# First rows normed beside the modulation, GpSimd's pieces of the attention reordered, and the last norm scaled through a diagonal on TensorE

## What is computed

```python
m_lat = silu(c) @ w_mod + b_mod            # six vectors: sh1 sc1 g1 sh2 sc2 g2; m_ctx from c_ctx likewise
h = modulate(x, sh1, sc1)                  # (x - mean) / std * (1 + sc1) + sh1, context rows with their own
u, gate, q, k, v = split(h @ w_in)         # 512, 512, 512, 128, 128
r = rglru(conv(u));  a = window_attention(rope(q), rope(k), v, context keys, sink)
y = concat(rms_norm(r * gelu(gate)), rms_norm(a)) @ w_out
x1 = layer_norm(ALPHA * x + g1 * y, ln1);  h2 = modulate(x1, sh2, sc2)
out = layer_norm(ALPHA * x1 + g2 * moe(h2), ln2)   # 32 experts, top 1 group, top 2 experts
```

## Time and profile before

| what | value |
|---|---|
| median of 3 runs | 2081.2 us (2080.24 to 2082.03) |
| the profiled execution's own time | 2081.28 us |
| its span | 2079.5 us |
| TensorE matmuls / VectorE / ScalarE / GpSimd busy | 82% / 70% / 51% / 25% of the span |
| mean granted TensorE clock | 0.923 of full |
| projection, attention, output, route blocks start near | 68.9, 578.4, 829.4, 1082.9 us |
| combine block starts near | 2014.7 us |

### The profile page before, as it was taken

The page is one execution under the profiler, slowest core; times in us unless marked ns, Lnnn a source line. Parts: engine busy times, 40 slices in busy tenths (PEclk is TensorE's granted clock), DMA queues, the critical chain, the costliest instruction groups (busy, mean ns, idle before and its releaser), DMA issues. The chain is left out here.

```text
span 2079.5 us, 76106 instructions
## 1 busy us (share of the span) xinstructions
PE 1713.2 (82%) x31174; PEld 1373.2 (66%) x31176; DVE 1464.5 (70%) x1828; ACT 1066.5 (51%) x1378; POOL 526.5 (25%) x413
## 2 busy tenths in 40 slices
PE   3488888888669997899961689986899799999947
PEld 0266666434257776455541689986899799999932
DVE  2466766388869997788878747777888636578727
ACT  2234343577558886433311535566676435456626
POOL 0000000000047777333322113231323121233213
PEclk7599999999889999899975899998999899999979
DMA  9321211367363331344326576898999748879837
GB/s 375 104 92 56 96 60 52 129 229 259 122 251 124 115 121 40 125 153 159 136 91 223 196 242 206 266 361 316 352 373 342 263 137 280 270 228 368 272 77 278
DMA packets 167293, 412.59 MB, mean 198 GB/s; under 512 B 15977, under 2 KB 24625, under 8 KB 165553
## 3 DMA queue, kind: packets, MB, share of 16 engines
q1 hardware_dynamic: 155554, 369.14, 49.4%
q0 software_dynamic: 11664, 42.47, 8.3%
HBM read 343.38 MB, written 68.19 MB: 198 GB/s over the span
## 5 line engine op out<-in xcount | busy, mean ns | idle before, releaser
L2200 PE MATMUL ps<-arena 128*128 128x64 f16 x7680 | 708.5, 195 | 53.9 <-DVE arena L2121 25.7
L2200 PEld LDWEIGHTS ps<-arena 128*128 128x128 f16 x7680 | 686.5, 99 | 62.5 <-issue 50.4
L2201 PE MATMUL ps<-arena 128*128 128x64 f16 x7680 | 708.3, 195 | 4.7 <-issue 3.9
L2202 PE MATMUL ps<-arena 128*128 128x64 f16 x7680 | 708.2, 195 | 3.9 <-issue 3.0
L2201 PEld LDWEIGHTS ps<-arena 128*128 128x128 f16 x7680 | 686.2, 99 | 6.0 <-issue 5.0
L2202 PEld LDWEIGHTS ps<-arena 128*128 128x128 f16 x7680 | 686.3, 99 | 2.8 <-issue 2.7
L2121 DVE SCALAR_TENSOR_TENSOR arena<-arena 128x2048 f16<-128x2048 f32 (+1 forms) x232 | 457.6, 2012 | 162.9 <-ACT arena L2048 95.5
L2048 ACT ACTIVATE arena<-arena 128x2048 f16<-128x2048 f32 x192 | 359.0, 1904 | 126.3 <-DMA arena<-w 80.0
L644 PE MATMUL ps<-arena 128*128 128x256 f16 (+1 forms) x1680 | 237.7, 303 | 21.1 <-DVE arena L529 21.1
L644 PEld LDWEIGHTS ps<-arena 128*128 128x128 f16 x1680 | 165.8, 100 | 87.3 <-DVE arena L529 15.2
L2015 POOL COPY ix<-gidx 128x1 int32 (+1 forms) x40 | 47.0, 1176 | 531.3 <-DVE arena L2154 531.3
(11 more groups left out here) (308 smaller groups left out, 3107.6 us busy)
## 6 DMA issues: line engine op xcount, KB each, us to landing
arena<-w SPq DMA_DIRECT2D x192, 1024.0 KB, 12.0
arena<-hT_d SPq DMA_DIRECT2D x64, 512.0 KB, 6.2
arena<-w_mod SPq DMA_DIRECT2D x16, 1536.0 KB, 8.3
h_d<-arena SPq DMA_DIRECT2D x17, 512.0 KB, 3.0
x_d<-arena SPq DMA_DIRECT2D x17, 512.0 KB, 2.6
arena<-x SPq DMA_DIRECT2D x8, 1024.0 KB, 6.2
...
```

The costliest lines, as they stand in the source:

```text
L2200: pe.matmul(out, whi[lane][:, at:at + P], high, start=first, stop=False)
L2201: pe.matmul(out, whi[lane][:, at:at + P], low, start=False, stop=False)
L2202: return pe.matmul(out, wlo[lane][:, at:at + P], high, start=False, stop=last)
```

## The change

It does three things, and some that these need.

1. The context rows, the first latent rows, the taps and the tables are loaded in the modulation's block, behind the last slab of w_mod; VectorE takes the context rows' statistics there and scales them, and GpSimd makes their power. The split of w_in is done at one go, ahead of that; w_in is loaded in four groups of rows (2, 2, 3, 1 rows k, three transfers each) to other places in SBUF, and ScalarE starts when the first four rows k are there. The modulation is multiplied with 32 weight columns, 30 of them zero, so that the bias is added on all 128 partitions in two additions; TensorE transposes the result from SBUF in six 128x128 pieces, and VectorE writes the columns by seven small operations, without the way through DRAM. The zero rows are stored ahead of the second four slabs. The rows are still stored to DRAM, and SP waits for that in the attention's block, ahead of the load of g1.
2. GpSimd's order in the attention: two rows of w_out in each of pairs 0 to 3, gn in pair 4, the first piece of slab 7 at the end of pair 6, the other two in pair 7 between the two inverses. In the output phase ScalarE copies the late sums after the first tile's `prepare` and no longer first.
3. In the last norm ScalarE writes a diagonal matrix of 1/std (128x128) in place of the normalised tile, VectorE writes (x - mean) times the gain straight from x, and TensorE multiplies that by the diagonal. SP waits for VectorE's pass before it loads x t+4.

The diff, cut to its core. `from_one` semaphores are raised to `START` = 1 by GpSimd at the beginning. In the experts the semaphore `g_y_tr` is replaced by one of the attention's, with its count as offset.

```diff
+def norm_rows(nc, dve, g, x, s, landed):
...
+    dve.wait_ge(landed[0], landed[1])
+    for t in range(TPC):
+        for a in range(2):
+            nc.vector.bn_stats(st[:, t, a, :], x[:, t, a * 512:(a + 1) * 512]).then_inc(stats, 1)
...
+
+    def scale():
+        dve.wait_ge(rstd, START + s + 1)
+        for t in range(TPC):
+            nc.vector.tensor_scalar(x[:, t, :], x[:, t, :], mv[:, t, 0:1], rs[:, t:t + 1], ALU.subtract, ALU.mult).then_inc(normed, 1)
+    return scale
...
+            sp.wait_ge(rows_done, 1)
             for m in range(4):
-                sp.dma_start(rows[m], by_group[0][m]).then_inc(c_ld, 16)
+                sp.dma_start(row_of[m], by_group[0][m]).then_inc(c_ld, 16)
             for n in range(RING):
                 sp.dma_start(ring[n], slab(n)).then_inc(wmod_ld[n], 16)
             sp.dma_start(g["idn"][:], g["ident"]).then_inc(g["const_ld"], 16)
             w_in = g["w_in"].rearrange("(k p) n -> p k n", p=P)
-            for dst, src in ((0, 0), (D_RNN, D), (REST, D_RNN)):
-                size = QKV if src == D else D_RNN
-                sp.dma_start(raw[:, :, dst:dst + size], w_in[:, :, src:src + size]).then_inc(win_ld, 16)
+            first = 0
+            for at, count in RAW:
+                part = arena[:, at:at + count * D_IN].rearrange("p (k n) -> p k n", k=count)
+                for dst, src in ((0, 0), (D_RNN, D), (REST, D_RNN)):
+                    size = QKV if src == D else D_RNN
+                    sp.dma_start(part[:, :, dst:dst + size], w_in[:, first:first + count, src:src + size])\
+                        .then_inc(win_ld if first < KD // 2 else win_ld2, 16)
+                first += count
+            sp.wait_ge(rows_done, 2)
+            for table in (g["h2_d"], g["x1_d"]):
+                sp.dma_start(table[SEQ:SEQ + P, :], spare).then_inc(rows_st, 16)
             for n in range(RING, RING * HALVES):
                 sp.wait_ge(mod_mm, n - RING + 1)
                 sp.dma_start(ring[n % RING], slab(n)).then_inc(wmod_ld[n % RING], 16)
-            sp.wait_ge(rows_done, 1)
-            for table in (g["h2_d"], g["x1_d"]):
-                sp.dma_start(table[SEQ:SEQ + P, :], spare).then_inc(rows_st, 16)
-            sp.wait_ge(rows_done, 1 + 4 * HALVES)
+            sp.wait_ge(later("b_pads"), START + 1)
+            sp.dma_start(first_rows(arena, 0), g["ctx_x"].rearrange("(t p) d -> p t d", p=P)).then_inc(x_ld[0], 16)
+            sp.dma_start(first_rows(arena, 1), g["x"][0:TPC * P, :].rearrange("(t p) d -> p t d", p=P)).then_inc(x_ld[1], 16)
+            sp.dma_start(arena[:, PAR0:PAR0 + C_RNN * NPAR].rearrange("p (c n) -> p c n", n=NPAR),
+                         g["rg_par"].rearrange("(c p) n -> p c n", p=P)).then_inc(tab_ld, 16)
+            for at, src in ((COS0, "cos_t"), (SIN0, "sin_t")):
+                sp.dma_start(arena[:, at:at + T_LAT * 32].rearrange("p (n d) -> p n d", d=32), g[src].rearrange("n p d -> p n d"))\
+                    .then_inc(tab_ld, 16)
+            sp.wait_ge(rows_st, 32)
+            sp.wait_ge(rows_done, 2 + HALVES)
             for m in range(4):
-                sp.dma_start(by_group[1][m], rows[m]).then_inc(rows_st, 16)
-            sp.wait_ge(rows_st, 96)
+                sp.dma_start(by_group[1][m], row_of[m]).then_inc(rows_st, 16)
...
+            nc.gpsimd.memset(col["mh"], -0.5).then_inc(later("b_pads"), 1)
+            pool.wait_ge(later("b_pads"), START + 1)
+            pool.wait_ge(later("b_var"), START + 1)
+            nc.gpsimd.tensor_tensor(col["rs"], col["ve"], col["mh"], ALU.pow).then_inc(later("b_rstd"), 1)
...
+            act.wait_ge(rows_done, 2)
+            nc.scalar.activation(c2a.rearrange("p (k n) -> p k n", k=KD)[:, :, 0:2], c2s.rearrange("p (k s) -> p k s", s=2), ACT.Silu)\
+                .then_inc(silu_done, 1)
...
-            act.wait_ge(win_ld, 48)
             for k in range(KD):
+                if k == 0:
+                    act.wait_ge(win_ld, 96)
+                if k == KD // 2:
+                    act.wait_ge(win_ld2, 96)
                 for cols, (high, low) in halves:
-                    nc.scalar.activation(high[:, k, :], raw[:, k, cols], ACT.Copy, scale=W_SCALE).then_inc(win_hi, 1)
+                    nc.scalar.activation(high[:, k, :], raw[k][:, cols], ACT.Copy, scale=W_SCALE).then_inc(win_hi, 1)
...
-                            mm = pe.matmul(ps[32 * m:32 * m + 2, i, 0:NARROW], c2a[:, 2 * k:2 * k + 2],
+                            mm = pe.matmul(ps[32 * m:32 * m + 32, i, 0:NARROW], c2a[:, 32 * k:32 * k + 32],
...
+            pe.wait_ge(g["const_ld"], 16)
+            pe.wait_ge(rows_done, 2 + HALVES)
+            for i in range(HALVES):
+                for q in range(COLS):
+                    mm = pe.transpose(ps[:, 2 + i, q * P:(q + 1) * P], rows[:, i * NARROW + q * P:i * NARROW + (q + 1) * P], g["idn"][:])
+            mm.then_inc(later("b_mcol_tr"), 1)

         @block.vector
         def _(dve):
+            nc.vector.memset(rows, 0.0).then_inc(rows_done, 1)
+            nc.vector.memset(c2a, 0.0)
             nc.vector.memset(spare, 0.0).then_inc(rows_done, 1)
+            for k in range(KD):
+                dve.wait_ge(win_hi, 2 * k + 2)
+                for cols, (high, low) in halves:
+                    nc.vector.scalar_tensor_tensor(low[:, k, :], raw[k][:, cols], W_SCALE, high[:, k, :], ALU.mult, ALU.subtract)
+            scale = norm_rows(nc, dve, g, first_rows(arena, 0), 0, (x_ld[0], START + 16))
             dve.wait_ge(c_ld, 80)
+            dve.wait_ge(mod_mm, RING * HALVES)
             for i in range(HALVES):
-                dve.wait_ge(mod_mm, RING * (i + 1))
-                for m in range(4):
-                    nc.vector.tensor_tensor(rows[m][:, i, :], ps[32 * m:32 * m + 2, i, 0:NARROW], rows[m][:, i, :], ALU.add).then_inc(rows_done, 1)
-                for k in range(4 * i, 4 * i + 4):
-                    dve.wait_ge(win_hi, 2 * k + 2)
-                    for cols, (high, low) in halves:
-                        nc.vector.scalar_tensor_tensor(low[:, k, :], raw[:, k, cols], W_SCALE, high[:, k, :], ALU.mult, ALU.subtract)
+                part = rows[:, i * NARROW:(i + 1) * NARROW]
+                nc.vector.tensor_tensor(part, ps[:, i, 0:NARROW], part, ALU.add).then_inc(rows_done, 1)
+            scale()
+
+            sc_ok = later("b_sc")
+            dve.wait_ge(later("b_mcol_tr"), START + 1)
+            for s in range(2):
+                at = ps[:, 2:4, 0:NARROW].rearrange("p i (q m c) -> p c i m q", q=COLS, m=4)[:, s]
+                nc.vector.tensor_scalar(mcol[:, s, 0:12].rearrange("p (m q) -> p m q", q=COLS), at[:, 0], X_SCALE, None, ALU.mult)\
+                    .then_inc(sc_ok, 1)
+                nc.vector.tensor_scalar(mcol[:, s, 12:15], at[:, 1, 0], X_SCALE, None, ALU.mult).then_inc(sc_ok, 1)
+                nc.vector.tensor_scalar(mcol[:, s, 15:16], at[:, 1, 1, 0:1], X_SCALE, None, ALU.mult).then_inc(sc_ok, 1)
+            dve.wait_ge(sc_ok, START + 6)
+            nc.vector.tensor_scalar(mcol[:, :, KD:2 * KD], mcol[:, :, KD:2 * KD], X_SCALE, None, ALU.add).then_inc(sc_ok, 1)
...
-            sp.dma_start(x[0], x_ctx).then_inc(x_ld[0], 16)
-            sp.dma_start(x[1], x_lat[0]).then_inc(x_ld[1], 16)
-            for m in range(2):
-                sp.dma_start(mrow[2 * KD * m:2 * KD * (m + 1), :],
-                             g["mod_rows"][m:m + 1, 0:2 * D].rearrange("o (r p) -> (o r) p", p=P)).then_inc(tab_ld, 16)
...
-            act.wait_ge(sc_ok, START + 2)
+            act.wait_ge(sc_ok, START + 7)
...
-            with pool.Fori(0, LAST + 1) as s:
+            with pool.Fori(1, LAST + 1) as s:
...
             dve.wait_ge(pads, START + 8)
-            norm(0, 0)
-
-            dve.wait_ge(mcol_tr, START + 1)
-            dve.wait_ge(tab_ld, START + 16 * 5)
-            nc.vector.tensor_scalar(mcol[:, :, KD:2 * KD], mcol_ps[:, :, KD:2 * KD], 1.0, X_SCALE, ALU.add, ALU.mult).then_inc(sc_ok, 1)
-            nc.vector.tensor_scalar(mcol[:, :, 0:KD], mcol_ps[:, :, 0:KD], X_SCALE, None, ALU.mult).then_inc(sc_ok, 1)
-            dve.wait_ge(sc_ok, START + 2)
+            dve.wait_ge(tab_ld, START + 16 * 3)
...
-            pe.wait_ge(tab_ld, START + 16 * 5)
-            pe.transpose(ps[:, 2, 0:4 * KD], mrow, idn[0:4 * KD, 0:4 * KD]).then_inc(mcol_tr, 1)
...
+            sp.wait_ge(g["done"]["rows_st"], DONE["rows_st"])
...
+            def late_term(k, n):
...
-            for i in range(PAIRS):
-                inverse(i, 0)
-                late_terms(i, 0, 2)
-                inverse(i, 1)
-                late_terms(i, 2, LATE_P)
...
+            def gated_row(k):

                 pool.wait_ge(w_ld, START + 16 * 7)
-                row = arena[:, OUT_W0 + i * D:OUT_W0 + (i + 1) * D]
+                row = arena[:, OUT_W0 + k * D:OUT_W0 + (k + 1) * D]
                 nc.gpsimd.tensor_tensor(row, row, ow["g1"], ALU.mult).then_inc(w_gate, 1)
```

(52 more changed lines are left out.)

104 lines of the change are left out of this document (57 added, 47 removed).

## The result

| | before | changed |
|---|---|---|
| first comparison, medians of 4 runs each | 2080.72 us (2075.72 to 2082.03) | 2048.93 us (2046.54 to 2053.15) |
| ratio, 95% interval | | 0.9862 (0.9832 to 0.9892) |
| span of the profiled execution | 2079.5 us | 2047.1 us |

Faster, as forecast, but by 31.8 us and not by 23.0. One execution of the kernel before on the last chip (4446 us) is counted as slow and enters no ratio. I compare the two profiles block by block; a block's start is that of its first instruction in the trace.

A forecast was written before the change was run, and what follows sets the result against it. Bounds: transfers then a serial chain in the modulation, GpSimd ending the attention, a copy heading the output, VectorE in the last norm. Gains 11.7 + 3.7 + 2.8 + 4.8 = 23.0 off 2081.2 give 2058.2 us, range 2053.5 to 2064.5.

The forecast's parts named there:

- Front: Modulation up to ScalarE's first modulated piece: it starts at 69.8 instead of 81.48, -11.7 us, bounds -8 to -14.
- The small column operations: End of the front: seven operations on VectorE at no more than 0.20 us each, done at about 68.5.
- Attention: End of the attention block: it ends with SP's wait at 825.4 instead of GpSimd's work at 829.1, -3.7 us.
- the feared late steps: Attention: with GpSimd's idle cover gone, steps late by 2.4 us, five times, would turn the gain into +8.
- Output: Output projection: ScalarE starts 3.7 us earlier and gives back 0.8 for the moved copy, -2.8 us, bounds 0 to -3.7.
- Last norm: Last norm: 0.9 from spacing, 2.3 of 2.6 us waiting for x, 1.7 in the last step; -4.8, bounds +4 and -6.
- the last line of the sum: Whole kernel: the summed gain of 23.0 us taken from the median of 2081.2 gives 2058.2 us.
- 1: Front: x or the small-piece tables arrive late, 4 us less gain, 2062 us; chance 0.15 together with 6.
- 6: Attention: another late waiter ends the block where GpSimd did, 3.7 us lost, 2062; counted with 1, 0.15 together.
- 2: Last norm: transfers bound it, so only the last step's 1.7 of 4.8 us is gained, 2061.3 us; chance 0.12.
- 3: Output: the late rows arrive too late and take the output's gain, 2061 us; chance 0.05.
- 5: Output: longer TensorE wait drops its clock to 1.2 GHz, up to 14 us per token tile, 2100 at three; chance 0.02.

The follow-up runs named there:

- e9: The changed kernel with the context rows' load issued ahead of the last slab of w_mod instead of behind it; 2043.58 us, ratio 0.9879 to the kernel before.
- e11: The changed kernel with the two zero-row stores issued behind the first rows' load instead of ahead of w_mod slabs; 2046.71 us, ratio 0.9864 to the kernel before.
- e13: The kernel of e11 with the load of sin_t issued by ScalarE instead of SP; 2051.41 us, ratio 0.9877 to the kernel before.
- e1: The kernel before with only the experts' semaphore of the transposed rows renamed; 2067.98 us, ratio 0.9991.
- e3: The kernel before with only GpSimd's new order of late pieces and ScalarE's late copy behind the first weights; 2060.98 us, ratio 0.9951.
- e4: The kernel before with only the last norm of the change; 2064.70 us, ratio 0.9971.
- e5: The kernel before, unchanged, profiled once more; 2070.55 us.
- e7: The kernel before with only GpSimd's new order, ScalarE's late copy left at the head of the output block; 2066.17 us, ratio 0.9983.
- e8: The kernel before with only ScalarE's late copy moved behind the first weights, GpSimd's order as before; 2065.65 us, ratio 0.9987.
- e15: The kernel before, unchanged, profiled on the chip of e13 and e14; 2075.87 us, ratio 1.0004.
- e2: The kernel before with the modulation and projection edits, the semaphore, and SP's wait for stored rows in the attention; 2054.99 us, ratio 0.9926.
- e12: The kernel of e11 with the first rows loaded ahead of the last slab, as in e9; 2048.36 us, ratio 0.9873 to the kernel before.
- e14: The changed kernel once more, on a chip where the kernel before is slower; 2049.96 us, ratio 0.9873 to the kernel before.
- e6: The changed kernel again, beside the kernel before on the same chip; 2044.76 us, ratio 0.9886.

## Why the prediction was wrong, point by point

**The gain, block by block.** Thirteen profiles (all but e9 and e11 to e13, whose front is another) hold each seam in its old or its new form. Means:

| | old | new | difference | forecast |
|---|---|---|---|---|
| first product | 88.93 (8 profiles, 87.96 to 89.54) | 76.67 (5, 76.46 to 76.87) | -12.3 | -11.7 |
| first product to attention block | 488.9 (8) | 487.6 (5) | -1.3 | 0 |
| attention block | 250.60 (7) | 247.02 (6) | -3.6 | -3.7 |
| output block | 253.47 (7) | 250.50 (6) | -3.0 | -2.8 |
| last norm | 64.90 (8) | 60.44 (5) | -4.5 | -4.8 |

The sum is -24.6 (before rounding); I had 23.0. (First two rows: old is before, e1, e3, e4, e5, e7, e8, e15; new the changed kernel four times and e2.) The second row is within what executions of one code differ there: 486.3 to 491.2 in the old form.

**Front.** Right in mechanism and nearly in size. One term was missed: in the earlier trace rows the last slab's matmuls took 2.74 us, in e5 1.61, with a granted clock of 0.50 in the window 55 to 58 us of the one and 0.86 in 55 to 57 of the other. In the old order that difference reaches the first product (89.48 and 88.25). In the new one the statistics stand beside the matmuls, and the first product moves by 0.4 over five profiles. The small column operations took 0.54 from first to last start, not seven times 0.20: 0.7 of the 1.0 us by which the first piece beat the forecast.

**Attention.** Right. The barrier is where SP's last wait puts it, 2.16 us behind the last store's issue. None of the feared late steps shows: GpSimd still waited 0.21, 0.54, 0.54 and 0.52 us before its sums in steps 1 to 4.

**Output.** Right on the mean. With order and copy both new the block took 249.8 us in six profiles (249.77 to 249.86) and 251.5 to 251.9 in three (e3, e12, e14). In e14 the first normalisation stood 25.95 us behind the block's start instead of 24.26, behind TensorE; the granted clock of both stretches before it was 0.85 and 0.87. What separates the two I leave open.

**Last norm.** The size of two terms: waits of 1.0 us on x stayed, where I let 0.3 stand; spacing and last step were as computed.

**The step that failed** is the last line of the sum, 2081.2 - 23.0. I took the closeness of profiled execution and median, 0.1 us, as a sign that this base would come again, and made the range of the terms' bounds alone. The unchanged kernel took 2064 to 2085 us in later runs, its medians 2069.0 to 2075.9 by chip, and its experts block 867.5 to 880.1 in three profiles. The base was thus 5.4 to 12 us above later medians of the same kernel, and 7.9 of the 32.4 us between the two spans came from a block of the same code. "The rest is unchanged" does not say that it takes the same time.

An estimate of the shares of the 9.3 us: the changed kernel's 2048.9 us and its 51 idle pieces are those of the chips of e11 to e15 (2046.7 to 2051.4 us, 46 to 51 pieces), where the kernel before had medians of 2075.1 to 2075.9. From a base of 2075.5 the same result is a gain of 26.6 us. Then 5.7 of the 9.3 us come from the base, whose first executions would then have lain high by chance (argued, not shown), 1.6 from the blocks of the table above, and 2.0 from no block that I can name.

**The size that remains.** The mean of the four ratios is (0.9862 + 0.9886 + 0.9860 + 0.9873)/4 = 0.9870, 27 us of 2075. The ledger gives 24.6 and the forecast 23.0, 0.9889, which three of the four intervals contain; that e6 came out at 0.9886 is partly luck. The parts alone gave 15, 9 to 10 (6 as e7 and e8) and 5 to 6 us, 26 to 31 in sum, each with about 3 us of uncertainty. So 2 us between ledger and times stay unexplained; the experts on chips like that of e15 are the candidate that is not excluded. The granted clock does not order the executions: e15 has 2072.19 us at a mean of 0.935 and 2082.09 at 0.939.

**The rivals.** 1 and 6 did not come: the tables landed in time and no other waiter held the attention. 2 did not: the spacing was 2.94, with a DMA share of 0.92 from 2006 to 2016 us. 3 held VectorE for 1.88 us that TensorE's wait covered. 5 did not come: the earlier trace rows's wait of 1.65 grew only to 1.86 before output tile 1.
